# A two-block transformer kernel on one core: the opening's weight loads, its modulation step and one reordering on VectorE

## What is computed

```python
silu_c, silu_cc = jax.nn.silu(c), jax.nn.silu(c_ctx)
mod_lat = split((silu_c  @ w_mod + b_mod), 6)      # w_mod is 1024 x 6144
mod_ctx = split((silu_cc @ w_mod + b_mod), 6)
h_lat = rmsnorm(x,   norm_mix_g) * (1 + mod_lat[1]) + mod_lat[0]
h_ctx = rmsnorm(ctx, norm_mix_g) * (1 + mod_ctx[1]) + mod_ctx[0]
lat, ctx = split_cols(h_lat @ w_in), split_cols(h_ctx @ w_in)   # w_in is 1024 x 8256
# attention (MLA), a two-way gated linear recurrence (HGRN2), both merged,
# a 32-expert MoE, and then the second block (RWKV7 + RG-LRU + MoE)
```

## Time and profile before

| | us |
|---|---|
| time before, median of 3 runs | 2201.53 (2201.14 to 2204.37) |
| the profiled execution | 2203.47 |
| its span in the trace | 2202.2 |
| TensorE busy in it | 2045.3 (93%) |
| first product with `w_in` starts at | 55.01 |
| first `z` product (load 5) starts at | 139.87 |

### The profile page before, as it was taken

One profiled execution on the slowest core, in us unless ns is written; L12 is line 12 of the kernel. 1 busy time (PEld: TensorE's weight loads), 2 busy tenths in 40 slices (PEclk: granted clock), 3 DMA queues, 4 the chain that ended last, 5 costly groups with the idle time before them and its releaser, 6 DMA issues.

```text
span 2202.2 us, 22437 instructions
## 1 busy us (share of the span) xinstructions
PE 2045.3 (93%) x9478; PEld 1075.9 (49%) x9478; DVE 732.3 (33%) x1230; ACT 294.1 (13%) x644; POOL 156.8 (7%) x207
## 2 busy tenths in 40 slices
PE   3989999999999999999999999999889999989997
PEld 1654467856453333333333333333368898553332
DVE  2177758435221111111101111111159544332213
ACT  1111130122021011111101111110024121110000
POOL 3122511010000000000000000000020100000100
PEclk7999999999999999999999999999989999989999
DMA  7598720131738999999999999999932212739995
GB/s 278 225 410 340 295 77 23 45 128 57 267 141 375 396 428 427 427 428 428 428 428 427 428 427 427 427 428 427 378 113 87 106 39 92 310 141 421 420 422 209
DMA packets 91992, 648.59 MB, mean 295 GB/s; under 512 B 10032, under 2 KB 15384, under 8 KB 47568
## 3 DMA queue, kind: packets, MB, share of 16 engines
q1 hardware_dynamic: 87216, 640.41, 70.8%
q0 software_dynamic: 4672, 6.68, 1.0%
HBM read 645.94 MB, written 1.11 MB: 294 GB/s over the span
## 4 chain that ended last, share of the span: by engine, by line
PE 76%; DMA 16%; DVE 3%; ACT 2%; issue 1%; POOL 0%; SPq 0%; POOLq 0%; DVEq 0%; ACTq 0%
PE ps L218 34%; PE ps L1661 14%; DMA sb<-in_w_down 8%; PE ps L1688 7%; DMA sb<-in_w_gate_up 6%; PE ps L2563 5%; PE ps L1404 5%; PE ps L2587 3%; PE ps L1650 2%; PE ps L223 2%; PE ps L604 2%; DMA sb<-in_w_in 1%; PE ps L621 1%; PE ps L2035 1%; DVE sb L973 1%
## 5 line engine op out<-in xcount | busy, mean ns | idle before, releaser
L218 PE MATMUL ps<-sb 128*128 128x128 f32 (+4 forms) x3782 | 827.1, 381 | 35.9 <-DMA sb<-in_w_in 10.2
L218 PEld LDWEIGHTS ps<-sb 128*128 128x128 f32 (+1 forms) x3782 | 578.9, 193 | 271.5 <-issue 213.8
L1661 PE MATMUL ps<-sb 128*64 128x512 f32 x2048 | 449.9, 596 | 1.3 <-DMA sb<-in_w_gate_up 0.6
L1661 PEld LDWEIGHTS ps<-sb 128*64 128x64 f32 x2048 | 143.8, 137 | 305.2 <-issue 291.7
L1688 PE MATMUL ps<-sb 128*64 128x512 f32 x1024 | 233.8, 612 | 49.6 <-DMA sb<-in_w_down 28.3
L1778 DVE TENSOR_SCALAR sb<-ps 128x512 f32<-128x512 f32 x32 | 33.6, 1049 | 491.6 <-PE ps L1661 491.6
L1688 PEld LDWEIGHTS ps<-sb 128*64 128x64 f32 x1024 | 87.5, 140 | 185.1 <-issue 185.1
L1415 DVE TENSOR_TENSOR sb<-ps,sb 128x512 f32<-128x512 f32 x64 | 44.3, 692 | 383.9 <-PE ps L1688 294.7
L1744 ACT COPY sb<-ps 128x512 f32<-128x512 f32 x32 | 18.8, 586 | 787.5 <-PE ps L223 787.5
L2563 PE MATMUL ps<-sb 128*64 128x512 f32 x512 | 114.4, 600 | 4.3 <-POOL sb L2660 3.7
L1404 PE MATMUL ps<-sb 128*128 128x512 f32 x256 | 115.3, 593 | 1.7 <-DVE sb L1415 1.7
(11 more groups left out here) (338 smaller groups left out, 1144.6 us busy)
## 6 DMA issues: line engine op xcount, KB each, us to landing
sb<-in_w_gate_up SPq DMA_DIRECT2D x128, 2048.0 KB, 23.8
sb<-in_w_down SPq DMA_DIRECT2D x64, 2048.0 KB, 26.3
sb<-in_w_in SPq DMA_DIRECT2D x24, 2048.0 KB, 8.3
sb<-in_w1e SPq DMA_DIRECT2D x32, 1024.0 KB, 16.0
sb<-in_w3e SPq DMA_DIRECT2D x32, 1024.0 KB, 18.1
sb<-in_w2e SPq DMA_DIRECT2D x32, 1024.0 KB, 19.9
sb<-in_w_ada SPq DMA_DIRECT2D x24, 1024.0 KB, 8.9
sb<-in_w_mod SPq DMA_DIRECT2D x16, 1024.0 KB, 12.2
```

The costliest lines, as they stand in the source:

```text
L218: last = te.matmul(o, l, r, start=i == 0, stop=i == len(pairs) - 1)
L1661: last = te.matmul(ps[64 * h:64 * h + 64, 512 * c:512 * c + 512], xg[k][:, t, 64 * m:64 * m + 64], w[:, at:at + 512], start=False, stop=t ...
```

## The change

It moves and rewrites steps of the first 120 us. Eleven places of the file are touched (the first one only renames a semaphore and is left out).

```diff
@@ -228,7 +228,9 @@
         SC0, MODTOP = K0 + 256, COLS - 3 * 4096
         mtmp = sb[:, MODTOP - 128 * (M_N + 4):MODTOP]
         modsb = Arena(sb, MODTOP - 128 * (M_N + 4) - 1024, MODTOP - 128 * (M_N + 4))
-        brow, mrow = modsb.take(512), modsb.take(512)
+        modsb.take(512)
+        mrow = modsb.take(512)
+        brow = sb[0:1, 28672:30720]
         ctmp = Arena(sb, K0 + 128, K0 + 152).take(3, 8)
         rows = Arena(sb, K0, K0 + 128).take(128)
         P0 = Arena(sb, SC0, MODTOP)
@@ -316,13 +318,14 @@
 
         NS = 7
         slots = [sb[:, COLS - 4096 * (i + 1):COLS - 4096 * i] for i in range(NS)]
-        r0 = SlotTable(slots, [0] * NS, ids=range(3))
+        first_places = {3: sb[:, 16384:20480], 4: sb[:, 20480:24576], 5: sb[:, 24576:28672], 2: slots[2]}
+        r0 = SlotTable(first_places, [0] * NS, ids=(3, 4, 5, 2))
         w_in = rows8(I["w_in"])
         mod_src = [I["w_mod"]] * 3 + [I["w_ada_2"]] * 3 + [I["w_ada_f_2"].unsqueeze(0)]
 
         for q in range(4):
             w = mod_src[0].rearrange("a (p t) n -> (a p) t n", t=8)
-            r0.add(two, w[:, 2 * q:2 * q + 2, 0:2048], (s["mod_w"], q + 1) if q < 3 else full_at(("mod", -1)))
+            r0.add(two, w[:, 2 * q:2 * q + 2, 0:2048], full_at(("mod", -1)))
         r1 = SlotTable(slots, r0.after(), ids=(1, 0))
 
         def add_cols(w, at, width, last_use):
@@ -444,15 +447,10 @@
             sp.dma_start(con, cf).then_inc(s["con"], 16)
             for n in range(4):
                 load(n, r0)
-            sp.wait_ge(*read_at(("mod", -1)))
-            for j in range(4):
-                sp.dma_start(mod1[:, 512 * j:512 * j + 512], mrow[32 * j:32 * j + 2]).then_inc(s["mod_first"], 16)
-            sp.wait_ge(s["mod_first"], 64)
-            for v in range(2):
-                sp.dma_start(mcol[:, v, 0:2], mod1[v, 0:2048].rearrange("(m p t) -> p m t", m=2, t=8)).then_inc(s["mcol1"], 16)
-            sp.dma_start(mtmp, cm).then_inc(s["cm"], 16)
             load(0, r1)
             load(1, r1)
+            sp.dma_start(mtmp, cm).then_inc(s["cm"], 16)
+            sp.wait_ge(*full_at(("mod", -1)))
             m = 0
             for n, upto in zip(range(2, 20), (5, 6, 9, 14, 16, 23, 30, 37, 44) + (48,) * 99):
                 while m < upto:
@@ -470,15 +468,19 @@
 
         def modulate_first(q):
             w = weights(q, r0)
+            o = P(("mod", -1))
             if q == 0:
-                opened(("mod", -1))
-            o = P(("mod", -1))
+                te.wait_ge(s["b_mod"], 16)
+                for j in range(4):
+                    te.matmul(o[32 * j:32 * j + 2, :], ones[0:1, 0:2], brow[:, 512 * j:512 * j + 512], start=True, stop=False,
+                              tile_position=(0, 32 * j))
             for tt in range(2):
                 for j in range(4):
                     last = te.matmul(o[32 * j:32 * j + 2, :], ccol[:, 0:2, 2 * q + tt],
-                                     w[:, tt, 512 * j:512 * j + 512], start=q == 0 and tt == 0, stop=q == 3 and tt == 1,
+                                     w[:, tt, 512 * j:512 * j + 512], start=False, stop=q == 3 and tt == 1,
                                      tile_position=(0, 32 * j))
-            last.then_inc(s["mod_w"] if q < 3 else is_full(("mod", -1)), 1)
+            if q == 3:
+                last.then_inc(is_full(("mod", -1)), 1)
 
         def modulate(r):
             te.wait_ge(s["msum"], 8 * r + 8)
@@ -524,7 +526,8 @@
             te.wait_ge(s["rows"], 16 * len(row_src))
             o = opened("rows")
             tr(o[:, 0:128], rows).then_inc(is_full("rows"), 1)
-            te.wait_ge(*read_at(("hT", 7)))
+            for t in (6, 7):
+                te.wait_ge(*read_at(("hT", t)))
             w = weights(next(order), r1)
             by_token(256, [("ckv", i) for i in range(4)], w)
             o = opened("kr")
@@ -743,6 +746,23 @@
             squares(x, stat[:, 0:16], 1024)
             ac.wait_ge(s["ctx"], 16)
             squares(big, stat[:, 16:32], 1024)
+            o = filled(ac, ("mod", -1))
+            ac.copy(mrow[64:66], o[64:66, :])
+            ac.wait_ge(s["mod01"], 2)
+            ac.copy(mrow[96:98], o[96:98, :]).then_inc(is_read(("mod", -1)), 1)
+            ac.wait_ge(*read_at(("mod", -1)))
+            for j in range(4):
+                ac.dma_start(mod1[:, 512 * j:512 * j + 512], mrow[32 * j:32 * j + 2]).then_inc(s["mod_first"], 16)
+            ac.wait_ge(s["mod_first"], 64)
+            for v in range(2):
+                ac.dma_start(mcol[:, v, 0:2], mod1[v, 0:2048].rearrange("(m p t) -> p m t", m=2, t=8)).then_inc(s["mcol1"], 16)
+            ac.wait_ge(s["mod01"], 6)
+            for t in range(0, 8, 2):
+                o = filled(ac, ("hT", t))
+                for k in range(2):
+                    last = ac.activation(hT[:, t, 256 * k:256 * k + 256], o[:, 256 * k:256 * k + 256], ACT.Identity,
+                                         bias=ab[:, 2 * k + 1, t:t + 1], scale=ab[:, 2 * k, t:t + 1])
+                last.then_inc(is_read(("hT", t)), 1)
             for i in range(4):
                 o = filled(ac, ("ckv", i))
                 ac.copy(ckv[:, i, :], o[:, 0:256]).then_inc(is_read(("ckv", i)), 1)
@@ -859,9 +879,7 @@
                     .then_inc(s[f"b_late{r % 2}"], 16)
 
         def pool_mix1():
-            for j in range(4):
-                for v in range(2):
-                    gp.dma_start(brow[32 * j + v:32 * j + v + 1, :], I["b_mod"][:, 512 * j:512 * j + 512]).then_inc(s["b_mod"], 16)
+            gp.dma_start(brow, I["b_mod"][:, 0:2048]).then_inc(s["b_mod"], 16)
             for i, n in enumerate(("norm_mix_g", "norm_ffn_g", "g_mix_2", "g_ffn_2")):
                 gp.dma_start(gcol[:, i, :], I[n].rearrange("a (p t) -> (a p) t", t=8)).then_inc(s["gains"], 16)
             gp.wait_ge(s["con"], 16)
@@ -918,8 +936,9 @@
 
 
         def scale_shift(i, v, m, g):
-            ve.scalar_tensor_tensor(ab[:, 2 * i, :], mcol[:, v, m + 1, :], 1.0, gcol[:, g, :], ADD, MUL).then_inc(dv.up(), 1)
-            ve.tensor_copy(ab[:, 2 * i + 1, :], mcol[:, v, m, :]).then_inc(dv.up(), 1)
+            ve.scalar_tensor_tensor(ab[:, 2 * i, :], mcol[:, v, m + 1, :], 1.0, gcol[:, g, :], ADD, MUL) \
+                .then_inc(s["mod01"] if i < 2 else dv.up(), 1)
+            ve.tensor_copy(ab[:, 2 * i + 1, :], mcol[:, v, m, :]).then_inc(s["mod01"] if i < 2 else dv.up(), 1)
 
         def hgrn_scan(d):
             gs = gss[d]
@@ -988,16 +1007,15 @@
                         .then_inc(s["xn"], 1)
             ve.memset(rows, 0.0).then_inc(s["rows0"], 1)
             o = filled(ve, ("mod", -1))
-            ve.wait_ge(s["b_mod"], 128)
-            for j in range(4):
+            for j in range(2):
                 r = slice(32 * j, 32 * j + 2)
-                ve.tensor_tensor(mrow[r], o[r, :], brow[r], ADD).then_inc(is_read(("mod", -1)) if j == 3 else dv.up(), 1)
+                ve.tensor_copy(mrow[r], o[r, :]).then_inc(s["mod01"], 1)
             ve.wait_ge(s["mcol1"], 32)
             ve.wait_ge(s["gains"], 64)
             scale_shift(0, 0, 0, 0)
             scale_shift(1, 1, 0, 0)
-            ve.wait_ge(s["dve"], dv.n)
-            for t in range(8):
+            ve.wait_ge(s["mod01"], 6)
+            for t in range(1, 8, 2):
                 o = filled(ve, ("hT", t))
                 for k in range(2):
                     ve.tensor_scalar(hT[:, t, 256 * k:256 * k + 256], o[:, 256 * k:256 * k + 256], ab[:, 2 * k, t:t + 1],
@@ -1019,13 +1037,13 @@
             s1, s2 = lbs[:, :, 0, :], lbs[:, :, 1, :]
             ve.wait_ge(*read_at("rows"))
             ve.tensor_tensor(s1, lg[:, :, 0, :], lg[:, :, 1, :], SUB).then_inc(s["lb0"], 1)
+            for m in range(2, 8):
+                add_half(m)
             ve.wait_ge(s["lb1"], 1)
             ve.tensor_scalar(s1, s1, -0.25, 0.25, MUL, ADD).then_inc(dv.up(), 1)
             ve.wait_ge(s["dve"], dv.n)
             ve.tensor_scalar(s2, s1, -1.0, 1.0, MUL, ADD).then_inc(dv.up(), 1)
             t_lb = dv.n
-            for m in range(2, 8):
-                add_half(m)
             for f in range(8):
                 if f % 2 == 0:
                     add_half(8 + f // 2)
```

More of the change, by code:

```diff
@@ L130 @@
 SEMS = """c x ctx con cm b_mod gains rows0 rows more wr b_late0 b_late1 mod_out0 mod_out1 mod_first mcol1 ctanh cc sq rstd
-    xn dve pool mask mod_w msum mrow lb0 lb1 qt zf qh kg KG st_half hg_ks hg_up kr hgn z_qr osum gt qn qrn scmx mg ymd x_mix
+    xn dve pool mask mod01 msum mrow lb0 lb1 qt zf qh kg KG st_half hg_ks hg_up kr hgn z_qr osum gt qn qrn scmx mg ymd x_mix
     row2 mcol
```

## The result

| | before | after |
|---|---|---|
| median | 2201.91 us (20 runs) | 2205.78 us (20 runs) |
| ratio after / before | | 1.0022, interval 1.0014 to 1.0029 |
| profiled execution / its span | 2203.47 / 2202.2 | 2201.82 / 2200.4 |
| T0, first product with `w_in` | 55.01 | 62.29 |
| Z, first `z` product | 139.87 | 141.75 |

Its profiled execution happened to be the second shortest of its 20 (2199.68 to 2207.95), so the profile's span is no measure of the loss; the landmarks inside it are.

What follows compares the result with a forecast made beforehand. TensorE bounds the kernel (76% of the span), so only its idle stretches up to the first `z` product count. Opening +6.4 and sums -6.3 give +0.1 us, 2201.6 us against the median; range 2192 to 2207.

Steps and rivals of the forecast that it cites:

- two large terms: Opening up to T0 loses 6.4 us, T0 to Z gains 6.3 us; sum +0.1 us.
- A: The forecast: trip's reads go one for one with SyncE's packets, ending at 57.2; 2201.6 us, range 2198 to 2205, chance 0.47.
- Four places, bias, copies: First modulation: `w_mod` places and bias matmuls 0, copies out of PSUM on two engines; ready at 39.85 instead of 40.72, 0.9 gained.
- Writes: Trip's small writes to DRAM beside queued loads: 0.94 to issue, 5.1 us to land, at 45.9.
- Reads: Trip's 32-byte reads: 34 turns against 8 KB packets, 10.9 us from 46.35 to 57.2, when SyncE's queue also runs dry.
- B: Rival: one 5.1 us delay for the trip's whole bunch of reads, ending near 51.5; -5.6 us, 2195.9, chance 0.28.
- C: Rival: ScalarE's queue is not held up, trip ends at 44.3, T0 48.5; -12.8 us in all, 2188.7, chance 0.10.
- T0: First product with `w_in`: trip's end 57.2 plus 0.43, 3.66 for columns and 0.1 gives 61.4, 6.4 us lost.
- D: Rival: queue moves at 359 GB/s, slowing the drain, then the 12.6 MB; +7.7 us, 2209.2, deciding at 380 GB/s, chance 0.15.
- T0 to Z: Sums ahead of `lb` let loads through load 5 stream without a hole: 78.6 us instead of 84.9, 6.3 gained.
- From Z to the end: TensorE is fed without countable gaps from 140 us on, so a shift of Z passes whole to the end.
- the frame: Z's shift passes whole to the end; called wrong if Z and the end move by amounts over 2 us apart.

Runs made afterwards that it cites:

- run 1: The changed kernel with loads m 0 to 3 issued only when the trip's reads have landed; 2195.91 us, ratio 0.9977 to before.
- run 7: The changed kernel with the masks and m 0 to 2 ahead of `w_in` 1, so the reads meet 2 KB packets; 2201.28 us, ratio 0.9995 to before.
- run 4: The changed kernel with the DRAM trip on SyncE's queue, behind `w_in` 0, 1 and masks, ahead of m 0 to 3; 2197.15 us, ratio 0.9976 to before.
- run 5: The changed kernel with only `w_in` 0 ahead of the trip; masks, `w_in` 1 and m 0 to 3 behind its reads; 2191.02 us, ratio 0.9955 to before.
- run 2: The kernel before with only sums m 2 to 7 moved ahead of VectorE's wait for ScalarE's tanh; 2197.97 us, ratio 0.9987 to before.
- run 3: The changed kernel with sums m 2 to 7 back behind the two `lb` steps; 2207.91 us, ratio 1.0034 to before.
- run 6: The changed kernel without the DRAM trip: 32 small matmuls turn the row pairs into columns in PSUM; 2193.54 us, ratio 0.9965 to before.
- run 9: The kernel of run 5 once more, unchanged, beside run 8 on the same chip; 2190.06 us, ratio 0.9942 to before.
- run 8: The kernel of run 5 with m 11 to 13 queued behind load 5, the first of `z`; 2183.42 us, ratio 0.9913 to before.

## Why the prediction was right or wrong

The time, 2205.78, lies in the range 2192 to 2207, and two large terms nearly cancel, as forecast. It is the edge of what I had expected: outside A's own range (2198 to 2205), and with a ratio of 1.0022 just beyond the 0.2% up to which I had called it the same, with a chance of 0.50, against 0.15 for slower. Against the +0.1 us of the forecast the medians moved by +3.9: 1.8 us of the difference stand at Z (0.9 in T0, 0.9 from T0 to Z), and 1.7 behind it in the profiled execution.

- **Four places, bias, copies.** Predicted ready at 39.85; it was 38.3. The fourth load landed at 33.18 instead of 34.18 (I took 0, at best 0.5), its matmuls took 3.04 instead of 3.64, the two pairs of copies 2.0 instead of 2.84 (predicted 1.97). No run took these edits singly.
- **Writes.** Predicted 5.1, from the one row with a small write beside loads; it was 6.82 in after, and 5.20 to 7.35 in the other runs with loads beside it, 8.47 behind the loads in SyncE's queue. Mis-sized by 1.7, and made up for by the earlier start: they landed at 46.26, predicted 45.9. They too go by turns: after 2.5 us without a packet, 16 packets follow in two strands of eight, each time behind one of the 14 KB packets of `cm`, 0.57 us apart, 3.9 us in all.
- **Reads.** 10.94 after the last issue, predicted 10.9, and that the two agree is in part luck. One packet for one is right (runs 1 and 7), but 34 such turns did not fill the time: 3.1 us passed before the first packet, for which I had nothing, and the turns were cut short when SyncE's queue ran dry. In full they would have taken about 3.1 + 10.9 = 14 us (an estimate from the two). What set the landing is the other half of my sentence, the end of the 9.44 MB: 57.2 predicted, 57.65 measured. Why nothing moves for 3.1 us beside loads is open. The Trainium skill (DMA: Bandwidth & Descriptors, Queues, rings and completion order) gives a packet 9 to 17 descriptors, by which, as an estimate, the reads would have gone in two to four turns. The rows do not agree with it: they show one 32-byte run in each turn. Rivals B and C fell with runs 1, 4 and 5; C's 48.5 for T0 is what run 5 gives, by taking the neighbours away.
- **T0.** 61.4 predicted, 62.29 measured, so +7.3 and not +6.4: 0.45 from the trip, 0.1 from the eight steps of columns (3.77 for 3.66), 0.3 from the 0.42 us between the last `hT` tile and the first product, for which I had 0.1.
- **D's rate.** The drain ran at 381 GB/s and not 410, at D's deciding point of 380. It hardly showed, since it also began 1.0 us earlier. From 109 us on the rate was 401 to 421, so the second half of D did not come.
- **T0 to Z.** 78.6 predicted, 79.46 measured, so 5.4 gained and not 6.3. Load 3 to Z took 32.1 us for the 12.6 MB instead of 31.4, and T0 to the first product with load 3 took 47.4, 0.2 more than before. No wait at `modulate(0)`, as predicted; runs 2 and 3 confirm the mechanism.
- **From Z to the end.** This step failed, and with the 1.9 us at Z it is what the profile shows of the loss: I let a shift of Z pass whole. Z came 1.9 us late; the first product of L607 came 3.6 late (329.50 against 325.93). The difference is the clock. In before, TensorE had been at the lower level (1.2 GHz) for a part of `hq` 4 to 7, with a clock of 0.91, and load 5 was late anyway, so it cost nothing. In after, the stretch at the lower level came right behind the 3.03 us wait at Z:

```profile
141.70:185.00 43.30, 43.25 (x100) 18.86 (x104) 27.90 (x21) 3.03 (x6) 12.25 (x12) 0.96 0.90 357
```

There 96 products took 43.16 us, in before and in run 2 the same 96 took 41.47: 1.7 us, and nothing hides it. +7.3 - 5.4 + 1.7 = +3.6, beside +3.9 in the medians.

What stays open: where the lower level falls. It followed Z's wait in after and in runs 1, 4, 6, 7 and 9, but not in 2, 3 and 5 (in 3 it had come ahead of Z, as in before), and 5 and 9 are the same program. The profiled execution of after was 4.0 us late at 656 us and only 0.7 late at 721; its mean granted clock was 0.95 from 656 to 690 us and 1.00 from 690 to 722, that of before 0.90 and 0.95. The medians do not give this back. By the sign that I had set, that Z and the end should not move by amounts more than 2 us apart, the frame holds only just by the medians (+1.9 and +3.9) and fails between the two profiled executions (+1.9 and -1.8). So a single execution's landmarks are good to some 2 to 4 us here, and my +3.6 agreeing with +3.9 is partly luck.

All runs against their own runs of before (Z's shift, plus 1.7 where the lower level followed it):

| run | Z's shift | with the clock | time |
|---|---|---|---|
| after | +1.9 | +3.6 | +3.9 |
| 1 | -6.5 | -4.8 | -5.5 |
| 2 | -5.6 | -5.6 | -3.5 |
| 3 | +8.1 | +8.1 | +6.5 |
| 4 | -6.9 | -5.2 | -4.3 |
| 5 | -12.3 | -12.3 | -11.3 |
| 6 | -11.5 | -9.8 | -8.7 |
| 7 | -3.8 | -2.1 | -1.0 |
| 8 | -15.7 | -15.7 | -19.5 |
| 9 | -12.6 | -10.9 | -12.9 |

The frame holds within about 2 us, but not for run 8, which gained 3.8 us more than its Z says.

## What to carry to other kernels

Before queuing loads early, ask what small transfer somebody waits for will share the DMA with them: two queues went turn by turn here, one packet each, so a reordering in 32-byte runs pays up to one large packet for every run (one in 16 of them on each DMA engine), after some 3 us in which nothing moves, until the other queue runs dry. Put such a trip before the bulk, or in the bulk's own queue ahead of what isn't needed yet, and let only what is needed first stand in front (run 5, which differs from after in the order of a few issues: -11.3 us instead of +3.9). A step that only produces something small, like the two steps of `lb`, should stand behind the work that frees buffers, since a wait on its engine is handed through semaphores to the loads (4.2 us at `modulate(0)`, 5.6 us at Z in run 2).

## What the runs showed of the hardware that was not expected

- Turns are by packet and blind to size: 32-byte packets went 328 to 330 against 7.4 KB ones and 409 to 431 against 2 KB ones.
- Issuing far ahead can hold the issuer. In after SyncE was held at the issue of `w_in` 0 and 1 for 22.28 us, where the same two took 1.95 in before; the queue did not run empty for it, and nobody waited:

```profile
6.40 22.28 SPq L438 DMA_DIRECT2D sb<-in_w_in  x2
```

- Small writes beside a full queue took 5.20 to 7.35 us from their last issue, with the DMA empty 1.24. In after 2.5 us of the 6.82 passed before the first packet, and 3.9 with turns behind 14 KB packets.
- Beside a full queue the first packet of the reads came 3.1 us after their last issue in after and in runs 3 and 7, 0.6 us with the DMA empty (runs 1 and 5). Why is open.
- The same program can have or not have 3.4 us of TensorE at the lower clock level behind a 3 us wait; it is worth 1.7 us, of the order of the effect measured here. Runs 5 and 9 are such a pair: 96 products in 41.47 us and in 43.16. Run 9, after its wait at Z, with a clock of 0.96 for the stretch; run 8, with no wait there, 1.00:

```profile
127.00:170.30 43.30, 43.07 (x96) 18.75 (x96) 28.04 (x21) 2.98 (x5) 12.42 (x12) 0.96 0.90 357
```

```profile
124.00:167.00 43.00, 43.00 (x108) 18.63 (x107) 34.93 (x28) 6.15 (x11) 12.52 (x12) 1.00 1.01 403
```
